# First mixer of a two-block network: another order of its work, one-pass forget sums, and probabilities scaled ahead of their transposes

## The reference

```python
h = h + even_mixer(rms_norm(h, norm_mix[0]), ...)

def even_mixer(hn, w_in, conv_w, conv_b, ga_w, ga_b, gx_w, gx_b, lam, f_b, w_out):
    proj = hn @ w_in                                     # 1024 -> 2568
    xr, yr, q, k, v, f_logit = jnp.split(proj, EVEN_SPLITS, axis=-1)
    xc = causal_depthwise_conv(xr, conv_w, conv_b)       # width 4
    h_lru = rglru(xc, ga_w, ga_b, gx_w, gx_b, lam)
    y_a = h_lru * jax.nn.gelu(yr)
    log_f = jax.nn.log_sigmoid(f_logit + f_b)
    y_b = fox_attention(q, k, v, log_f)                  # 8 heads of 64
    return jnp.concatenate([y_a, y_b], axis=-1) @ w_out

def rglru(x, ...):
    r = sigmoid(block_diag(x, ga_w, ga_b)); i = sigmoid(block_diag(x, gx_w, gx_b))
    log_a = -8.0 * r * softplus(-lam)
    a = exp(log_a); u = sqrt(-expm1(2.0 * log_a)) * (i * x)
    return scan(h = a * h + u)

def fox_attention(q, k, v, log_f):                       # per head, blocks of 128 queries
    c = jnp.cumsum(log_f, axis=1)
    logits = (q * dh ** -0.5) @ k.T + c[query] - c[key]
    p = softmax(where(query >= key, logits, -inf))
    return p @ v
```

## Time and profile before

| | |
|---|---|
| median of three runs | 2533.14 us (2533.14 to 2536.32) |
| profiled execution | 2535.88 us, its span 2534.2 us, granted clock 0.993 |
| busy in the span | PE 98%, PEld 83%, DVE 80%, ACT 61%, POOL 3% |
| first mixer, unit 0 to last out part | about 12.5 to 146.4 us |
| in it (12 to 146.5 us) PE busy | 125.5 us of 134.5 |

### The profile page before, as it was taken

How to read it: one execution, slowest core, us unless ns; L and a number is a source line. 1 busy time by engine, 2 the same in 40 slices (tenths; PEclk the granted TensorE clock), 3 DMA queues, 4 the chain that set the end, 5 groups by cost and what they waited for, 6 DMA issues and landing times.

```text
span 2534.2 us, 39606 instructions
## 1 busy us (share of the span) xinstructions
PE 2476.1 (98%) x14338; PEld 2110.1 (83%) x14338; DVE 2027.9 (80%) x2919; ACT 1534.1 (61%) x2127; POOL 67.1 (3%) x152
## 2 busy tenths in 40 slices
PE   9899999899999999999999989999999999999998
PEld 8688887788888888888888878889888888898887
DVE  5577764689899989998999977789877777798776
ACT  5554453477777777777777764463544544544543
POOL 8000000000000000000000000000000000000000
PEclk9999999999999999999999999999999999999999
DMA  7256643399999999999999976643466566433663
GB/s 207 92 160 190 183 134 132 101 364 375 352 359 372 365 359 358 371 371 353 361 372 365 371 216 189 186 124 110 147 197 189 165 195 195 144 102 113 192 195 102
DMA packets 481899, 597.31 MB, mean 236 GB/s; under 512 B 21882, under 2 KB 313154, under 8 KB 481760
## 3 DMA queue, kind: packets, MB, share of 16 engines
q1 hardware_dynamic: 478048, 589.47, 69.7%
q0 software_dynamic: 3712, 6.00, 0.8%
HBM read 594.35 MB, written 1.05 MB: 235 GB/s over the span
## 4 chain that ended last, share of the span: by engine, by line
PE 91%; DVE 5%; ACT 2%; issue 1%; DMA 1%; SPq 0%; ACTq 0%; DVEq 0%
PE bank L812 24%; PE bank L618 16%; PE bank L654 12%; PE bank L838 12%; PE bank L624 8%; PE bank L603 5%; PE bank L600 2%; PE bank L1452 1%; PE bank L981 1%; PE bank L823 1%; PE bank L1150 1%; DVE wlo_ring L2096 1%; PE bank L874 1%; PE bank L759 1%; PE bank L634 0%
## 5 line engine op out<-in xcount | busy, mean ns | idle before, releaser
L2096 DVE TENSOR_TENSOR wlo_ring<-raw_ring,whi_ring 128x1024 fp32r<-128x1024 f32 (+1 forms) x1122 | 1328.7, 1220 | 127.3 <-ACT whi_ring L1502 109.1
L1502 ACT CAST whi_ring<-raw_ring 128x1024 fp32r<-128x1024 f32 (+1 forms) x1122 | 1143.0, 1052 | 164.8 <-DMA raw_ring<-in_od_exp_w_dram 150.3
L618 PE MATMUL bank<-x,whi_ring 128*128 128x512 f32 x1720 | 428.3, 391 | 0.0
L618 PEld LDWEIGHTS bank<-x,whi_ring 128*128 128x128 f32 x1720 | 315.6, 188 | 60.7
L624 PEld LDWEIGHTS bank<-x,wlo_ring 128*128 128x128 f32 x1720 | 220.8, 191 | 8.4
L624 PE MATMUL bank<-x,wlo_ring 128*128 128x256 f32 x1720 | 223.5, 283 | 0.0
L1566 ACT COPY arena<-bank 128x256 f32<-128x256 f32 x110 | 40.9, 372 | 283.9 <-PE bank L624 283.9
L603 PE MATMUL bank<-x,whi_ring 128*128 128x256 f32 (+2 forms) x1024 | 193.8, 290 | 0.9 <-DVE x L2166 0.9
L812 PE MATMUL bank<-whi_ring,xg0hi 128*128 128x512 f32 x448 | 177.7, 397 | 0.8 <-issue 0.8
L812 PE MATMUL bank<-whi_ring,xg1hi 128*128 128x512 f32 x448 | 177.2, 396 | 0.0
L812 PE MATMUL bank<-whi_ring,xg0lo 128*128 128x512 f32 x448 | 174.9, 390 | 0.0
(11 more groups left out here) (514 smaller groups left out, 3446.9 us busy)
## 6 DMA issues: line engine op xcount, KB each, us to landing
raw_ring<-in_od_exp_w_dram SPq DMA_DIRECT2D x672, 512.0 KB, 5.4
raw_ring<-in_ffn_w_gate_dram SPq DMA_DIRECT2D x88, 512.0 KB, 4.0
raw_ring<-in_ffn_w_up_dram SPq DMA_DIRECT2D x88, 512.0 KB, 4.9
raw_ring<-in_ffn_w_down_dram SPq DMA_DIRECT2D x88, 512.0 KB, 3.5
raw_ring<-in_ev_ffn_w_dram SPq DMA_DIRECT2D x66, 512.0 KB, 3.9
raw_ring<-in_w_in_dram SPq DMA_DIRECT2D x42, 512.0 KB, 4.0
raw_ring<-in_od_w_in_dram SPq DMA_DIRECT2D x24, 512.0 KB, 3.8
raw_ring<-in_ev_w_in_dram SPq DMA_DIRECT2D x20, 512.0 KB, 6.4
```

Source lines behind the costliest of these rows:

```text
L618: mm_ = mm(bank[:, :], wh[:, kt, :], X2[:, kt, :, :].rearrange("p a n -> p (a n)"), start=(start and kt == 0), stop=(stop and kt == KT - 1 ...
L1502: nc.scalar.copy(WHI[:, slot, 0:n], RAW[:, slot, 0:n]).then_inc(s["hi_ready"], 1)
L2096: V_.tensor_tensor(WLO[:, slot, 0:n], RAW[:, slot, 0:n], WHI[:, slot, 0:n].bitcast(F32), ALU.subtract)\
```

## The change

Only the first mixer and what is made for it change.
- The forget sums of the keys go through TensorE in one pass. GpSimd makes a wider selector `SEL2` (one memset, four selects on 32 partitions each); VectorE rounds it into `SELR`, writes the negated forget gates four times into `LFP`, and evicts the cumulative sums for all 128 partitions into `NCTR`, with their rounding rests in the partitions from 32 and from 96. `scores` starts with this matmul.
- Probabilities are scaled by VectorE ahead of their transposes (`normalized`). The matmuls that spread reciprocals, and `scaled`, are gone; `hi` and `lo` read the values' results from their banks (`PVB`).
- TensorE: scores 0 and 1 stand ahead of unit 13; the wait for the columns stands inside step 0; the gates are announced in two halves.
- VectorE: most low parts (`ahead`) stand elsewhere, one of them inside the convolution instead of four, and six spread over steps 0 to 7; the low part of chunk 1 stands ahead of the x parts; the squares of `AE` go over XR. ScalarE: chunk 2 is cast behind the x parts, unit 13 is evicted behind the first two exps, kt = 0 to 3 are split one step earlier.

On TensorE, behind unit 12, before: the transposes of parameter rows (L932) and the sixteen matmul pairs of unit 13 stand ahead of this, which is the end of unit 13, scores 0 and 1 (L993, L995) and the start of unit 14.

The diff, without the list of semaphore names and with little of its context:

```diff
@@ -260,12 +260,17 @@
         SPX, SPE, SPN, SPR, SPS, SPP, SP = (c(20) for _ in range(7))
-        NCT = c(S, parts=8)
+        c.at += -(ARENA_AT // 4 + c.at) % 128
+        SELR, NCTR = (nc.alloc_sbuf_tensor_at(name, [P, *dims], F32R, offset=ARENA_AT + 4 * c.at + 4 * at)
+                      for name, at, dims in (("selr", 0, (8, P)), ("nctr", 8 * P, (S,))))
+        c.at += 8 * P + S
+        LFP = c(TT, P)
+        SEL2 = TH.rearrange("p a b -> p (a b)").rearrange("p (h q) -> p h q", h=8)
...
         AMX, ASUM, AREC = c(16), c(16), c(16)
-        PVS = c(4, S)
+        PVB = (BANK[6][:, 0:S], BANK[7][:, 0:S], BANK[0][:, 0:S], BANK[0][:, S:2 * S])
@@ -483,8 +488,11 @@
             link(nc.gpsimd.memset(SEL[:, :, :], 1.0))
+            link(nc.gpsimd.memset(SEL2[:, :, :], 1.0))
...
             select(SEL[:, :, :], ALU.is_equal, 0.0, [[1, 8], [0, P]], 0, -1)
+            for o in (0, 32, 64, 96):
+                select(SEL2[o:o + 32, :, :], ALU.is_equal, 0.0, [[1, 8], [0, P]], 0, -1)
@@ -943,10 +951,10 @@
                 pe.wait_ge(s["small_ready"], 1)
-                lf = SP[:, 4:20].rearrange("p (t h) -> p t h", t=TT)
-                mm(BANK[2][0:8, 0:P], lf[:, 0, :], UPPER[:, :], start=True, stop=True)
-                mm(BANK[2][0:8, P:S], lf[:, 0, :], ONES[:, :], start=True, stop=False)
-                mm(BANK[2][0:8, P:S], lf[:, 1, :], UPPER[:, :], start=False, stop=True)
+                lf = LFP[:, :, 0:8]
+                mm(BANK[2][:, 0:P], LFP[:, 0, :], UPPER[:, :], start=True, stop=True)
+                mm(BANK[2][:, P:S], LFP[:, 0, :], ONES[:, :], start=True, stop=False)
+                mm(BANK[2][:, P:S], LFP[:, 1, :], UPPER[:, :], start=False, stop=True)
@@ -958,14 +966,13 @@
                                   start=True, stop=True)
-                last.then_inc(s["gates_mm"], 1)
+                    last.then_inc(s["gates_mm"], 1)
...
                 turn_columns(1, 3)
-                u(13)
@@ -990,14 +997,13 @@
                     wait(pe, "bank_free", pr["q0"] + 12 + 2 * (h // 2))
+                    mm(BANK[2 + v % 2][:, 0:S], SELR[o:o + 64, h, :], NCTR[o:o + 64, :], start=True, stop=False, skip_group_check=True)
                     mm(BANK[2 + v % 2][:, 0:n], Q[o:o + 64, h // 2, t * P:(t + 1) * P], K[o:o + 64, h // 2, 0:n],
-                       start=True, stop=False)
-                    mm(BANK[2 + v % 2][:, 0:n], SEL[:, h, :], NCT[:, 0:n], start=False, stop=True)\
-                        .then_inc(s["score_ready"], 1)
+                       start=False, stop=True, skip_group_check=True).then_inc(s["score_ready"], 1)
...
                     t = v % 2
-                    pe.wait_ge(s["prob_ready"], v + 1)
+                    pe.wait_ge(s["pn_ready"], v + 1)
@@ -1009,32 +1015,26 @@
                     if v == 12:
-                        pe.wait_ge(s["pv_in"], 6)
-                    bank = BANK[6 + h // 2] if v < 8 else BANK[0]
+                        pe.wait_ge(s["x_ready"], x_at + 7)
                     for b in range(t + 1):
-                        last = mm(bank[o:o + 64, t * P:(t + 1) * P], V[:, b, h * 64:(h + 1) * 64],
+                        last = mm(PVB[h // 2][o:o + 64, t * P:(t + 1) * P], V[:, b, h * 64:(h + 1) * 64],
...
                     last.then_inc(s["pv_ready"], 1)
-                    if v % 4 == 3:
-                        pe.wait_ge(s["pv_in"], v // 2)
-                        for k in range(v - 3, v + 1):
-                            o = 64 * (k // 2 % 2)
-                            last = mm(bank[o:o + 64, S + k % 2 * P:S + (k % 2 + 1) * P],
-                                      AREC[:, k:k + 1].broadcast_to([P, 64]), IDENT[:, :], start=True, stop=True)
-                        last.then_inc(s["recx_mm"], 1)
...
                 pe.wait_ge(s["cumev_ready"], 1)
-                pe.wait_ge(s["cols_ready"], 2)
...
                 scores(1)
+                u(13)
...
                         u(14 + v // 2, v % 2 * KT // 2, (v % 2 + 1) * KT // 2)
+                        if v == 0:
+                            pe.wait_ge(s["cols_ready"], 2)
...
                         if v == 12:
-                            pe.wait_ge(s["pv_in"], 4)
+                            pe.wait_ge(s["x_ready"], x_at + 6)
@@ -1743,8 +1743,8 @@
                     evict(6 + i, YR[:, i, :], ACT.Gelu_apprx_tanh)
-                act.wait_ge(s["gates_mm"], 1)
-                for g, name, b in ((RG, "ga_b", 4), (IG, "gx_b", 6)):
+                for n, (g, name, b) in enumerate(((RG, "ga_b", 4), (IG, "gx_b", 6))):
+                    act.wait_ge(s["gates_mm"], n + 1)
@@ -1762,8 +1762,6 @@
                 af(TH[:, :, :], TH[:, :, :], ACT.Sqrt).then_inc(s["root_ready"], 1)
-                evict(13, K[:, 1, :], ACT.Copy)
-                ahead(c0 + 17)
@@ -1785,6 +1783,8 @@
                 exps(1)
+                evict(13, K[:, 1, :], ACT.Copy)
+                ahead(c0 + 17)
@@ -1793,33 +1793,35 @@
                             evict(u, K[:, u // 2 - 5, :], ACT.Copy)
-                    if v == 8:
+                    if v == 7:
+                        act.wait_ge(s["chunk_used"], c0 + 21)
...
                     copy(v)
+                    if v == 12:
+                        act.wait_ge(s["pv_ready"], 12)
+                        hi(6, PVB[2])
+                    if v == 7:
+                        hi(1, YR[:, 1, :])
...
                     if v == 7:
-                        act.wait_ge(s["chunk_used"], c0 + 21)
+                        for kt in (2, 3):
+                            hi(kt, YR[:, kt, :])
                     if v == 8:
-                        for kt in range(1, 4):
-                            hi(kt, YR[:, kt, :])
...
                     if v == 10:
-                        act.wait_ge(s["pv_in"], 4)
-                        hi(4, PVS[:, 0, :])
-                        hi(5, PVS[:, 1, :])
+                        act.wait_ge(s["pv_ready"], 8)
+                        hi(4, PVB[0])
+                        hi(5, PVB[1])
                         ahead(oc + 2)
-                    if v == 14:
-                        act.wait_ge(s["pv_in"], 6)
-                        hi(6, PVS[:, 2, :])
...
                 ahead(oc + 6)
-                act.wait_ge(s["pv_in"], 8)
-                hi(7, PVS[:, 3, :])
+                act.wait_ge(s["pv_ready"], 16)
+                hi(7, PVB[3])
@@ -2045,7 +2047,7 @@
                 mean_square(t)
-            ahead(-1)
+            ahead(-2)
@@ -2439,6 +2441,9 @@
                 V_.scalar_tensor_tensor(SPN[:, :], SPX[:, :], -1.0, SPX[:, :], ALU.mult, ALU.min).then_inc(s["spx_ready"], 1)
+                dve.wait_ge(s["consts_ready"], 1)
+                V_.tensor_copy(SELR[:, :, :], SEL2[:, :, :])
+                link(V_.memset(LFP[:, :, :], 0.0))
@@ -2448,12 +2453,17 @@
                 link(V_.tensor_scalar(SPS[:, 0:4], SP[:, 0:4], 8.0, None, ALU.mult))
-                V_.tensor_scalar(SP[:, 4:20], SP[:, 4:20], -1.0, None, ALU.mult).then_inc(s["small_ready"], 1)
+                for t in range(TT):
+                    last = V_.tensor_scalar(LFP[:, t, :].rearrange("p (o z) -> p o z", o=4)[:, :, 0:8],
+                                            SP[:, 4 + 8 * t:12 + 8 * t].rearrange("p (o z) -> p o z", o=1)
+                                            .broadcast_to([P, 4, 8]), -1.0, None, ALU.mult)
+                last.then_inc(s["small_ready"], 1)
...
                 for j in range(4):
-                    ahead(c0 + 9 + j)
+                    if j == 2:
+                        ahead(c0 + 9)
@@ -2466,26 +2476,30 @@
                 dve.wait_ge(s["cum_ready"], 1)
-                V_.tensor_scalar(NCT[:, :], BANK[2][0:8, 0:S], -1.0, None, ALU.mult)
+                link(V_.tensor_scalar(NCTR[:, :], BANK[2][:, 0:S], -1.0, None, ALU.mult))
+                for o in (32, 96):
+                    V_.scalar_tensor_tensor(NCTR[o:o + 8, :], BANK[2][o:o + 8, 0:S], -1.0, NCTR[o:o + 8, :].bitcast(F32),
+                                            ALU.mult, ALU.subtract)
...
                 dve.wait_ge(s["cumev_ready"], 1)
-                ahead(c0 + 14)
+                squares = flat_(XR)[:, 0:4 * S]
+                for j in range(3):
+                    ahead(c0 + 10 + j)
...
                 link(V_.tensor_tensor(flat_(IG), flat_(IG), flat_(XC), ALU.mult))
-                ahead(c0 + 15)
+                ahead(c0 + 13)
                 dve.wait_ge(s["aexp_ready"], 4)
-                link(V_.tensor_tensor(flat_(RG), flat_(AE), flat_(AE), ALU.mult))
+                link(V_.tensor_tensor(squares, flat_(AE), flat_(AE), ALU.mult))
+                ahead(c0 + 14)
...
                 dve.wait_ge(s["aexp_ready"], 8)
-                V_.scalar_tensor_tensor(flat_(TH), flat_(RG), 1.0, flat_(TH), ALU.add, ALU.mult)\
+                V_.scalar_tensor_tensor(flat_(TH), squares, 1.0, flat_(TH), ALU.add, ALU.mult)\
                     .then_inc(s["root_in"], 1)
-                ahead(c0 + 16)
-                ahead(c0 + 17)
```

(45 more changed lines are left out.)

2 lines of the change are left out of this document (1 added, 1 removed).

## The result

The changed kernel takes **2518.39 us** (median of 2519.74, 2519.26, 2517.51, 2516.17) against 2533.14 for the kernel before. The ratio is 0.993, with a 95% interval from 0.991 to 0.995, so it is faster: by 14.7 us by the two medians, by 17.7 by the ratio (13 to 22 by its interval). The profiled execution took 2519.74 us with a span of 2518.0, 16.2 less than before.

The account below looks back on a forecast made before the run. The prediction took TensorE's chain to bound the first mixer, with the rest of the program behind it. Terms -1.1 + 1.6 - 1.7 - 3.7 - 3.5 - 3.7 = -12.1, taken as -12, gave 2533.14 - 12 = 2521.1 us, range 2516 to 2530.

Parts of the forecast that it names:

- to the first transposes: From the gates to turn_probs(0): ScalarE's chain starts earlier, transposes at 72.9 instead of 77.84; 3.7 us of new gain.
- v = 0 to 7: First half of the loop: cheaper pairs, fewer reciprocal matmuls and a shorter stall bring out part 0 to 96.6; 3.5 us gain.
- Start and selects: Front: unit 0 ends 1.1 us earlier, but four selects at 1.24 us each delay it; cumulative sums 0.5 us later.
- Rival 4: GpSimd's new selects meet VectorE and take three times as long, +10 us: 2531, no change; chance 0.07.
- Convolution: Ahead of the gates: three of four splits leave it, TensorE's 1.5 us of waits go, gates near 52.9; 1.7 us gain.
- The wait ahead of the transposes: Ahead of turn_probs(0): TensorE idles 1.8 us; the old wait of 2.4 ahead of the scores shrinks and moves there.
- A pair of steps: In the loop: 5.96 us instead of 6.59, forget sums taken at 0.2 each; four pairs give 2.5 us.
- The stall ahead of the output: Ahead of the first out part: falls from 2.3 to about 0.9 us, since kt = 0 is split right behind unit 17.
- v = 8 to 15: Second half of the loop to the end: 6.7 us gone, including 2.4 of half clock, against new waits; net 3.7 gain.
- The ring: At v = 8, 9, 10, splits behind logits make laps of 4.4 us against TensorE's 2.98; TensorE waits some 3.0.
- Rival 1: The ring and the 0.9 us stall cost nothing, so -16 us: 2517; chance 0.10.
- Rival 3: Half clock behind the wait at 71 us or one in the loop costs 1.3 to 3: 2522 to 2524; chance 0.14.

Follow-up runs that it names:

- order alone: Also spelled order_only: the changed kernel with the old attention (old forget sums and reciprocal matmuls), so only the new order; 2518.83 us, ratio 0.994 to before.
- lighter_ring: Changed kernel with casts and splits of two output chunks moved from v = 9 and 10 to 11 and 13, later ones a step later; 2514.23 us, one execution.
- cast_wait: cast_late with TensorE's wait for GpSimd's last constants moved from ahead of the second turn of the columns to behind the loop; 2518.03 us, one execution.
- the saving alone: Kernel before with both lighter attention pieces, moved lines in the old order except the split of kt = 6; 2530.81 us, ratio 0.999 to before.
- cast_late: Changed kernel with the wide selector's cast and VectorE's wait for GpSimd moved from ahead of unit 2's eviction to behind the convolution; 2517.83 us, one execution.
- old_norm: Changed kernel with only the old normalization back: reciprocal matmuls on TensorE and the product on VectorE, no scaling ahead of the transposes; 2515.05 us.

## Why the prediction was wrong, by its own steps

The stretches between the marks, as predicted and measured (moves in us):

| stretch | predicted | order alone | whole change |
|---|---|---|---|
| start to cumulative sums | +0.5 | -1.6 | -0.2 |
| to the gates | -1.7 | -1.7 | -1.8 |
| to the first transposes | -3.7 | -4.5 | -4.0 |
| v = 0 to 7 | -3.5 | -2.4 | -5.0 |
| v = 8 to the end | -3.7 | -4.1 | -5.6 |
| sum | -12.1 | -14.2 | -16.5 |

- **Start and selects: right mechanism, small sizes.** The start was worth 1.4 for 1.1. A new select took 1.14 with its hand-over (four in 4.54 us) for 1.24, `consts_ready` fired at 30.0 for 30.4, and the light attention costs the front 1.35 for 1.6. Rival 4 did not come: VectorE had next to nothing to run beside the selects. What little it had was slowed: an instruction with two inputs of 128x20 took 0.85 us at 27.57, 0.18 in the kernel before.
- **Convolution: right** (1.7 predicted, 1.7 and 1.9 measured), with a slip: 54.13 + 0.5 - 1.5 is 53.1 and not 52.9, so the 1.7 has 0.2 more than the wait that it names.
- **The wait ahead of the transposes: right** (1.8 predicted, 1.7 measured). The sum has no term for the half clock behind the old wait of 2.4, 1.7 us by the windows, though the earlier trace rows was read as a wait "paid twice". It needed none: these low grants ended by 77.2 us, from 77.1 on TensorE waited another 0.7 us for the first exp, and the chain of waits up to it ran over VectorE and ScalarE alone. At full clock TensorE would only have waited longer. The rows of before:

```profile
75.45 1.23 DVE wlo_ring L2096
...
76.67 0.27 DVE arena L2495
...
77.29 0.50 ACT arena L1783 x2
```

- **v = 0 to 7: two terms mis-sized, and a sum that does not close.** A pair of steps takes 2.86 + 1.63 + 0.23 + 0.31 + 0.43 + 0.36 = 5.82 for 5.96: the forget sums cost 0.31, which is inside the bounds but above the 0.2 taken, and Q·K fell by 0.2, which was not foreseen. The stall ahead of the output is 0.36 for 0.9. The prediction's own terms (2.5 for the pairs, 0.44, and 1.4 for the stall) add up to 4.3, and it took 3.5 with no term for the 0.8 between. Measured: 3.1 for the pairs, 0.4 and 1.9, less a new wait of 0.4 at 86.3 us, 5.0.
- **v = 8 to 15: the step that missed most, by two terms mis-sized.** The ring cost 1.4 us of waits, not 3.0: three laps took 3.7, 4.1 and 4.2 us (logits at 96.59, 100.29, 104.43 and 108.67) for 4.4 each, which is the plain sum of the pieces, with nothing taken off for their overlap. The mechanism stands by lighter_ring, its size does not. And the clock behind the output's two waits took 3.4 (0.24 of it while TensorE still stood idle), not 2.4: the sum priced the slower out parts (2.90 and 2.65 for 1.59) and left out the transposes and Q·K behind the second one, which took 0.43 and 0.96 for 0.22 and 0.62.

By the table, the order alone was undervalued by 2.8 us (14.2 for 11.4): 0.5 in the front, 0.8 up to the first transposes, 1.0 in v = 0 to 7, where the stall went to nothing and not to 0.9, and 0.6 behind, where the clock's term was 1.0 too small. What gave the 0.8 stays open. On top of the order the light attention was worth 2.3 for 0.7: the ring was put 1.6 too dear and the pairs 0.6, and other parts, which no run separates, take some of that back. Rival 1, with the ring free, gave 16 and comes nearest in size, for another reason: the ring is not free. Rival 3 did not come in the changed kernel, but cast_wait shows how near it was. Behind the mixer nothing changed its length against before.

## What to carry to other kernels

Price a removed wait as the wait plus the whole stretch of low grants behind it, summed window by window; a stretch was 1.7 us behind waits of 2.4, 2.3 and 1.1 in the kernel before and up to 5.1 in others. Then follow the chain of waits: low grants that end ahead of a wait for another engine, as the first 1.7 here, cost nothing. Test an order and a saving of work apart: here the order alone gave 14.2 of the 16.5 us, the saving alone 3.4, and one of its parts cost 1.4 until the waits beside it were taken out. Before an instruction is moved on VectorE, look at what GpSimd runs beside it and who waits for that.

## What the runs showed of the hardware that I had not expected

- A TensorE matmul that uses other rows than the one ahead (128, then 64, then 8) took 0.20 us more, in one pass or several, and whichever of two stood first, also where the rows of the two had none in common; on the same rows nothing.
- Each stretch of low grants behind a wait lost 1.7, 3.4 or 5.1 us in all these mixers, nothing in between; the kernel before had three of 1.7. Waits of 2.6 and 3.5 us at one place cost 5.1 and 3.4 of it.
- A wait of 1.7 us was followed by full grant in the changed kernel and by 1.7 us of loss in cast_wait, in two executions of two; one of 1.1 us in the kernel before and two of 0.4 and 0.6 us in cast_late were followed by it as well.
- Behind the mixer, where all these kernels are the same, the low grants differed too: 10.4 us lost in the changed kernel, 7.0 in order_only, old_norm and lighter_ring, summed over windows of 20 us. Behind the mixer the changed kernel's execution is 3.3 us longer than order_only's (2388.1 and 2384.8), about these 3.4, and so order_only's time is within 0.5 us of the changed kernel's although its mixer is 2.3 longer. The difference lies in two places: 1.8 us from 1460 to 1480 (0.91 against 1.00), and 1.4 in this window, first of the changed kernel and then of order_only:

```profile
420.00:440.00 20.00, 17.39 (x68) 13.88 (x68) 11.90 (x17) 9.77 (x16) 0.00 (x0) 0.84 0.44 140
```

```profile
420.00:440.00 20.00, 16.68 (x74) 13.65 (x75) 13.42 (x20) 9.77 (x16) 0.00 (x0) 0.91 0.51 159
```
